# A retention layer's eight sample states: scaled and updated in their own buffers, v spread by one matmul, key tiles added before the query

## What is computed

```python
def step(s, inp):
    qc, kc, vc = inp
    ...
    s = g_c[None, :, None, None] * s + jnp.einsum('bmhk,bmhv->bhkv', kc * zeta[None, :, :, None], vc)
    return s, o
...
mu = jnp.mean(o, axis=-1, keepdims=True)
var = jnp.mean(jnp.square(o - mu), axis=-1, keepdims=True)
o = (o - mu) * lax.rsqrt(var + GN_EPS)
o = o.reshape(B, L, hv) * jax.nn.silu(g.astype(jnp.float32))
return o.astype(xn.dtype) @ w_out, s
```

## Time and profile before

| | us |
|---|---|
| median of 3 runs (2123.94 to 2133.53) | 2125.17 |
| the profiled execution | 2112.8 |
| its span, first to last instruction | 2111.0 |
| TensorE busy, matmuls | 1927.5 (91%) |
| VectorE busy | 1088.6 (52%) |
| ScalarE busy | 813.1 (39%) |
| GpSimd busy | 781.0 (37%) |
| mean granted TensorE clock | 0.938 |

### The profile page before, as it was taken

One profiled execution on the slowest core, in us unless ns is written; L12 is line 12 of the kernel. 1 busy time (PEld: TensorE's weight loads), 2 busy tenths in 40 slices (PEclk: granted clock), 3 DMA queues, 4 the chain that ended last, 5 costly groups with the idle time before them and its releaser, 6 DMA issues.

```text
span 2111.0 us, 32802 instructions
## 1 busy us (share of the span) xinstructions
PE 1927.5 (91%) x14440; PEld 1843.4 (87%) x14440; DVE 1088.6 (52%) x1074; ACT 813.1 (39%) x948; POOL 781.0 (37%) x230
## 2 busy tenths in 40 slices
PE   6989987899966999899999988999999988979998
PEld 6889877899955999898989978999989888879997
DVE  3344543576366764446363544675434544436753
ACT  3332232534425344444344434434532233144343
POOL 4334333545412544342212101355354334253552
PEclk9999997999977999999999978999999999889999
DMA  6657654355623555665454522455556655634452
GB/s 217 198 169 239 225 168 136 120 182 165 192 70 100 169 178 189 191 209 150 135 163 124 148 84 80 136 164 180 180 181 235 231 172 190 200 120 140 161 185 95
DMA packets 305764, 346.86 MB, mean 164 GB/s; under 512 B 7703, under 2 KB 269335, under 8 KB 305615
## 3 DMA queue, kind: packets, MB, share of 16 engines
q1 hardware_dynamic: 257696, 259.84, 38.8%
q10 hardware_dynamic: 47927, 84.93, 12.3%
HBM read 300.17 MB, written 44.82 MB: 163 GB/s over the span
## 4 chain that ended last, share of the span: by engine, by line
PE 80%; DVE 11%; ACT 4%; issue 2%; ACTq 1%; DMA 1%; POOL 0%; DVEq 0%
PE acc L1338 19%; PE acc L1339 19%; PE acc L1345 18%; PE mix L1451 5%; PE mix L1400 2%; PE mix L1442 2%; PE acc L1366 2%; PE acc L1367 1%; ACT w_hi L413 1%; PE acc L1372 1%; PE mix L1681 1%; PE mix L1720 1%; DVE k_stack L1004 1%; DVE w_lo L827 1%; PE mix L1653 1%
## 5 line engine op out<-in xcount | busy, mean ns | idle before, releaser
L1241 POOL TENSOR_TENSOR w_lo<-raw,w_hi 128x2048 fp32r<-128x2048 f32 (+2 forms) x162 | 691.7, 4274 | 886.1 <-ACT w_hi L413 886.1
L1338 PE MATMUL acc<-g_hi,w_hi 128*128 128x264 f32 x2588 | 666.2, 293 | 24.7 <-DVE y L871 11.3
L1339 PE MATMUL acc<-g_lo,w_hi 128*128 128x264 f32 x2588 | 654.4, 289 | 0.0
L413 ACT ACTIVATE w_hi<-raw 128x2048 fp32r<-128x2048 f32 (+3 forms) x260 | 455.7, 1754 | 391.3 <-issue 229.1
L1338 PEld LDWEIGHTS acc<-g_hi,w_hi 128*128 128x128 f32 x2588 | 497.5, 192 | 36.4 <-issue 25.1
L827 DVE TENSOR_TENSOR w_lo<-raw,w_hi 128x2048 fp32r<-128x2048 f32 (+2 forms) x98 | 381.8, 3896 | 272.5 <-ACT w_hi L413 272.3
L1339 PEld LDWEIGHTS acc<-g_lo,w_hi 128*128 128x128 f32 x2588 | 498.5, 193 | 1.4
L1345 PE MATMUL acc<-g_hi,w_lo 128*128 128x264 f32 x2588 | 347.4, 286 | 0.0
L1345 PEld LDWEIGHTS acc<-g_hi,w_lo 128*128 128x128 f32 x2588 | 330.7, 190 | 2.1
L1275 POOL TENSOR_TENSOR h_lo<-hid,h_hi 128x528 fp32r<-128x528 f32 x44 | 59.0, 1342 | 324.6 <-ACT h_hi L608 324.6
L1338 PE MATMUL acc<-h_hi,w_hi 128*128 128x264 f32 x664 | 164.1, 284 | 0.0
(11 more groups left out here) (220 smaller groups left out, 2381.6 us busy)
## 6 DMA issues: line engine op xcount, KB each, us to landing
raw<-in_w_ffn_in_dram SPq DMA_DIRECT2D x88, 1024.0 KB, 5.2
raw<-in_w_in_ret_dram SPq DMA_DIRECT2D x48, 1024.0 KB, 5.6
raw<-in_w_in_attn_dram SPq DMA_DIRECT2D x36, 1024.0 KB, 5.3
st_in<-in_state_ret_dram ACTq DMA_DIRECT2D x64, 512.0 KB, 4.8
out_dram<-st_out ACTq DMA_DIRECT2D x64, 512.0 KB, 3.4
raw<-in_w_ffn_out_dram SPq DMA_DIRECT2D x32, 768.0 KB, 4.3
raw<-in_w_ffn_out_dram SPq DMA_DIRECT2D x32, 640.0 KB, 4.0
raw<-in_w_out_ret_dram SPq DMA_DIRECT2D x16, 1024.0 KB, 5.1
```

The source lines that it names most:

```text
L413: A(w_hi[:, u % SPL, 0:size[u]], raw[:, u % RAW, 0:size[u]], ACT.Copy).then_inc(hi_split, 1)
L1241: TT(w_lo[:, u % SPL, 0:size[u]], raw[:, u % RAW, 0:size[u]], w_hi[:, u % SPL, 0:size[u]].bitcast(F32), ALU.subtract).then_inc(lo_by_pool, 1)
L1338: MM(out, wh, x_hi[:, ks[k], :], start=first and k == 0, stop=False)
L1339: MM(out, wh, x_lo[:, ks[k], :], start=False, stop=False)
```

## The change

st_in and st_out become five buffers `st`, in which a state stays from load to store. ScalarE multiplies it by gamma in place (`scale_to`). TensorE no longer makes k v^T but spreads v of one sample over all partitions with one matmul (`spread`, weights are one column of `sel` broadcast), alternating between the banks mix 2 and 3. VectorE's `update` adds it, times the key as a scalar of each partition (k_s, a copy of 8 columns of rk), for the two key tiles separately. For the query ScalarE multiplies the first key tile by the query's scalar (`t_first`, into the one buffer tq), VectorE adds the second (`t_last`), and TensorE sums tq over the partitions with a column of ones: 4 matmuls of one column instead of 8. A query now goes two samples behind the spread instead of one. k_stack, k_one, the transposes of the k row and v_stack's third and fourth parts are gone. The norm's sums go inside units 4 and 5; head 3's norm is cut into the prompt's 256 columns, which go along with the samples, and the samples' 8 columns ("late"). On ScalarE the hi split of units 4 and 5 comes ahead of the gate's silu, of which the second goes behind the outputs.

```diff
-            st_in = sb("st_in", [P, 3, 2, RDV], F32, s)
-            st_out = sb("st_out", [P, 2, 2, RDV], F32, s)
+            sel = sb("sel", [P, DECB], F32R, s)
+            k_s = sb("k_s", [P, 2, 2, DECB], F32, s)
+            tq = sb("tq", [P, RDV], F32, s)
+            st = sb("st", [P, ST, 2, RDV], F32, s)
...
 ScalarE
+                def load_to(end):
+                    for n in range(loaded[0], min(end, 32)):
+                        g = 32 * r + n
+                        if g >= ST:
+                            act.wait_ge(st_stored[g % ST], 16 * (g // ST))
+                            act.wait_ge(t_ready, g - ST + 1)
+                        act.dma_start(st[:, g % ST], st_view(state_ret, n)).then_inc(st_landed[g % ST], 16)
+                        loaded[0] = n + 1
+                def scale_to(end):
+                    for n in range(grown[0], min(end, 32)):
+                        g = 32 * r + n
+                        act.wait_ge(st_landed[g % ST], 16 * (g // ST + 1))
+                        A(st[:, g % ST], st[:, g % ST], ACT.Copy, scale=GAMMA[n // 8]).then_inc(st_scaled, 1)
+                        grown[0] = n + 1
+                def t_first(n):
+                    g = 32 * r + n
                     act.wait_ge(st_updated, g + 1)
+                    if g:
+                        act.wait_ge(qs_done, g)
+                    b = n % 8
+                    A(tq[:], st[:, g % ST, 0, :], ACT.Copy, scale=rq[:, n // 8 % 2, 0, SEQ + b:SEQ + b + 1])\
+                        .then_inc(t_first_ready, 1)
...
+                    for s in range(4):
+                        n = 8 * (h - 1) + 2 * s
+                        if h:
+                            load_to(n + 4)
                         if h or s:
                             hi(ub + s + 2)
+                        if h:
+                            if s:
+                                t_first(n - 1)
+                            store(n)
+                            load_to(n + 5)
+                            t_first(n)
+                            store(n + 1)
+                            scale_to(n + 4)
...
+                    if h:
+                        t_first(8 * h - 1)
+                    hi(ub + 6)
+                    if h:
+                        sample_out(gh - 1, 1 - par)
+                        load_to(8 * h + 4)
+                        gn_square(h - 1)
+                    gate_out(pb, 4, par)
...
+                    gate_out(pb, 5, par)
+                    act.wait_ge(s1_ready, gh + 1)
+                    act.dma_start(ret_p[r, 0, h].rearrange("(k p) v -> p k v", p=P), S0[:]).then_inc(s1_stored, 16)
+                    if h:
+                        ro_split(h - 1)
+                    scale_to(8 * h + 3)
...
+                    if b == 1:
+                        hi(uo + 2)
+                    if b == 5:
+                        hi(uo + 3)
+                    if b:
+                        t_first(n - 1)
+                    if b == 3:
+                        gn_square(3)
+                    if b == 6:
+                        gn_sqrt(3)
+                    store(n)
+                    load_to(n + 4)
+                    scale_to(n + 3)
...
 VectorE
+                def update(n):
                     g, b = 32 * r + n, n % 8
+                    dve.wait_ge(vb_done, g + 1)
+                    dve.wait_ge(st_scaled, g + 1)
+                    for kt in range(2):
+                        ins = STT(st[:, g % ST, kt, :], mix[:, 2 + g % 2, :], k_s[:, n // 8 % 2, kt, b:b + 1],
+                                  st[:, g % ST, kt, :], ALU.mult, ALU.add)
+                    ins.then_inc(st_updated, 1)
+                def t_last(n):
+                    g, b = 32 * r + n, n % 8
+                    dve.wait_ge(t_first_ready, g + 1)
+                    STT(tq[:], st[:, g % ST, 1, :], rq[:, n // 8 % 2, 1, SEQ + b:SEQ + b + 1], tq[:],
+                        ALU.mult, ALU.add).then_inc(t_ready, 1)
...
+                            update(n)
+                            if s:
+                                t_last(n - 1)
+                            update(n + 1)
+                            t_last(n)
+                        evac(s)
...
+                    if h:
+                        t_last(8 * h - 1)
+                        gn_first(h - 1)
+                        gn_center(h - 1)
+                    evac(4)
+                    if h:
+                        gn_second(h - 1)
+                    dve.wait_ge(v_stack_hi, gh + 1)
+                    TT(v_stack[32:40, :], mix[0:DECB, 2, :], v_stack[0:8, :].bitcast(F32), ALU.subtract)\
+                        .then_inc(v_stack_ready, 1)
+                    if h:
+                        gn_inverse(h - 1)
+                    evac(5)
...
 TensorE
+                def spread(n):
                     g, gh = 32 * r + n, RH * r + n // 8
...
+                    if g > 1:
+                        pe.wait_ge(st_updated, g - 1)
+                    MM(mix[:, 2 + g % 2, :], sel[:, b:b + 1].broadcast_to([P, P]), v_stack[:],
+                       start=True, stop=True).then_inc(vb_done, 1)
+                def query(n):
...
+                    pe.wait_ge(t_ready, g + 1)
+                    for vt in range(4):
+                        ins = MM(mix[:, 0, vt * 8 + b:vt * 8 + b + 1], tq[:, vt * P:(vt + 1) * P], ones[:, 0:1],
                                  start=True, stop=True)
                     ins.then_inc(qs_done, 1)
                 def sample(n):
+                    if n % 8 >= 2:
+                        query(n - 2)
+                    spread(n)
...
+                        if h and s < 4:
+                            samples = (lambda: sample(n), None, lambda: sample(n + 1))
+                        elif h and s == 4:
+                            samples = (lambda: query(8 * h - 1), None, lambda: gn_mean(h - 1))
+                        elif h:
+                            samples = (lambda: gn_variance(h - 1),)
...
+                proj(uo, po, ro_hi, ro_lo, first_half, last=False,
+                     between=(lambda: sample(24), lambda: second(25, gn_mean), lambda: sample(26)))
+                sample(27)
+                proj(uo + 1, po + 1, ro_hi, ro_lo, first_half, last=False,
+                     between=(lambda: sample(28), lambda: second(29, gn_variance), lambda: sample(30)))
+                sample(31)
+                pe.wait_ge(ro_lo_ready, 5 * r + 3)
+                proj(uo + 2, po, ro_hi, ro_lo, pieces[0], first=False, last=False, done=False,
+                     between=(lambda: query(30), None, lambda: query(31)))
+                proj(uo + 3, po + 1, ro_hi, ro_lo, pieces[0], first=False, last=False, done=False,
+                     between=(lambda: gn_mean(3, True), None, lambda: gn_variance(3, True)))
```

386 lines of the change are left out of this document (170 added, 216 removed).

## The result

The changed kernel took 2133.0 us in the median of 17 runs (2122.17 to 2141.35), the kernel before 2122.61 in 17 (2113.86 to 2133.53). The ratio is 1.0044 with a 95% interval of 1.0026 to 1.0062: slower by about 10 us, within the 0.5% (about 11 us) that the prediction called no change, though clear of 1.

What follows compares the result with a forecast made beforehand. TensorE was taken to bound the kernel, with 80% of the last-ending chain. Heads with samples +25, clock +18, first heads -9 and output stages -9 gave +25 us on the median of 2125.17: 2150 us, range 2120 to 2180.

Steps and rivals of the forecast that it cites:

- What decides, the lock: Sample units: t_last, with two SBUF inputs, waits for the end of GpSimd's w_lo under way, stopping TensorE's next query.
- each time: Sample units: t_last(n-1) always comes 0.6 us into a w_lo of 4.58 us.
- The ring, 12.9 us a unit: Units 1 to 3: chain from one blocked query to the next, 12.9 us, hiding TensorE's own 8.1; two layers +25 us.
- Load and gap 0.6: Units 1 to 3, ScalarE: 0.6 us for load issue and gap, counted between the two scalings and the hi split.
- Clock, +18: Heads with samples: after waits, query and spread run at a lower clock; 0 to 6 us a head, 3 taken, +18 us.
- First head with samples: First such head of a layer: no gn_last and ro_split ahead, so 76.8 us against 79.0 for the others.
- First head of a layer, -4.4 each: First head of each layer: the 3.03 us v_stack wait goes, L1521 gains 1.4 at full clock; -4.4 twice, -9 us.
- Output stage, -9: After the heads: two blocked t_last, but a short late norm chain; pieces at 54.5 instead of 58.9, -4.4 twice, -9 us.
- Cost at nothing: Memset of k_stack, k_s copy, and the five state buffers' loads in units 4 and 5: no time lost.
- The first rival: Sample units: t_last is not blocked, units of 8.9 us, heads of 60 us, 2015 us in all; chance 0.15.
- The second rival: Head ends: t_last blocked, but gn_first precedes w_lo (5 us less a head), full clock stays (3 less); 2100 us, chance 0.12.
- The clock stays at its lower level through the sample units: Rival, sample units: TensorE's 8.1 us become 16.2, +3 us for each of 18 units, 2200 us; chance 0.10.

Runs made afterwards that it cites:

- the memset: Changed kernel with GpSimd filling w_lo of the retention layers with zeros instead of subtracting, from the third unit on: 2009.37 us, ratio 0.9474.
- the order: Changed kernel with t_first(n-1) ahead of the hi split in units 1 to 3, nothing else moved: 2062.47 us, ratio 0.973.
- halves: Changed kernel with each w_lo of a retention layer made in two GpSimd instructions of 1024 columns: 2054.77 us, ratio 0.9678.
- quarters: Changed kernel with each w_lo of a retention layer made in four GpSimd instructions of 512 columns: 2023.67 us, ratio 0.9519.
- the norm-first run: Changed kernel with sample_out, and so gn_first, ahead of the hi split in unit 4, nothing else: 2112.71 us, ratio 0.9943.
- eighths: Changed kernel with t_first and sample_out ahead of the hi split everywhere and w_lo in eight parts of 256 columns: 2024.39 us, ratio 0.9563.

## Why the prediction was right and where it was wrong

It said slower, and by 25 us; it was slower by 10. The mechanism was there as described; what failed were sizes, the ring's cost and the output stage's clock. By its own steps:

- **What decides, the lock:** right. 28 of 64 t_last are long and end with a w_lo, and the memset, the order, and the halves and quarters show the cause one by one. Not "each time" at full length, though: a blocked t_last starts 0.57 to 2.5 us into its w_lo, and only 14 take over 4 us. Of the five waits of 3.8 to 5 us a head that were forecast, TensorE shows two in the second head (4.16 and 3.97), one in the third (4.16, then 2.65) and none in the first (2.09 at most). The gn_first that was to be blocked behind the hi of unit 4 is (4.78 us).
- **The ring, 12.9 us a unit:** too long, and this is the step that failed for the heads. Query 1 to query 3 is 12.3 us at full clock. "Load and gap 0.6" does not stand in the chain: the load's issue (171.49) lies inside the first scaling, with ScalarE working beside its own queue; and two scalings are 1.9, not 2.05. From query 0 to query 7 the forecast has 41.2 us at full clock and the trace 40.7, of which some 2.4 are the clock's (next point): about 3 us too much, some 17 over six heads if the ring is the same in all. By milestones from the end of the head before, forecast and measured: query 0 13.5 and 13.0, query 1 21.2 and 20.6, query 3 34.1 and 32.9, query 5 47.0 and 46.4, query 7 54.7 and 53.7, the mean 61.4 and 60.0, end 79.0 and 79.2.
- **Clock, +18:** about right in size in the second head, though its end came out as if the clock had cost nothing. Granted clock of TensorE in that head (stretch, its length, TensorE busy, clock, DMA share, GB/s):

```profile
166.00:180.00 14.00, 9.61 (x76) 0.99 0.69 245
180.00:186.00 6.00, 5.79 (x26) 0.50 0.89 302
186.00:193.60 7.60, 6.44 (x50) 0.96 0.51 175
193.60:201.00 7.40, 5.91 (x45) 1.00 0.82 286
```

  After the wait that ended at 180.21 the clock is at 1.2 GHz, and query 3 takes 1.87 us; after the shorter wait before 193.71 it is at 2.4, and query 5 takes 1.05. So the turn that starts at 180.21 is 13.5 us and the one at full clock 12.3, 1.2 more; this head has two such queries, 0 and 3. At the mean and what follows it come about 1 to 1.6 (17.6 forecast from the mean to the end, 19.2 measured). By this estimate the clock cost 3.4 to 4 us in this head against the 3 taken. With the same ring the first and third heads come to some 4 and 3. In this head the ring was over by as much, and the two hid each other: the end of 79.0 that was forecast at full clock was met at a mean clock of 0.89, and that is luck. The forecast with the clock, 82.0, was not met.
- **First head with samples:** forecast 76.8 before the clock and 79.8 with it, measured 74.7. Beside the ring's surplus query 0 came at 10.1 us (11.3 forecast), and the mean 4.7 us behind query 7 (6.7 forecast; gsq is held for 3.16 us here and not for 4.78). Three heads together: +21 a layer with the clock forecast, +9.7 and +10.5 measured. This is 22 us of the difference: by these estimates some 17 the ring, some 10 what comes before query 0 and between query 7 and the mean, less some 5 that the clock took beyond its +18.
- **First head of a layer, -4.4 each:** -5.1 and -4.5. Right.
- **Output stage, -9:** wrong in sign, +1, and this is the step that failed outside the heads. The clock was charged to the heads and not here, where it was lowest: 0.67 over the stage, with query 24 at 1.84 us. Query 24 came at 13.4 us (15.6 forecast), but query 31 at 53.0 (48), and the chain behind it to the first piece took 9.2 us where 6.5 was forecast. What was mis-sized is the samples between the blocked t_last, not the blocked step: query 24 to 27 took 15.7 us (11.4 forecast) and 28 to 31 16.3 (12.4), where 27 to 28 took 7.6 (8.6). The memset run, with no t_last blocked, has 13.8 and 15.5 for the same. At the lower clock query and spread are 2.5 us instead of 1.4; by that estimate the clock is some 1.1 us a sample, most of the difference. The pieces went at 62.2, not 54.5; what follows them won 2.5 back. This is 10 us the other way.
- **Cost at nothing** (k_s, the memset, the five buffers' loads): right. With t_last out of the way the sample units keep TensorE busy all the time at a DMA share of 0.81.

In sum: 25 - 22 + 10 - 1, about 12, against 11.6 in the two layers. The two wrong steps go opposite ways; that the total is no further off is luck too. The first rival, with no blocked t_last, was put at 2015 us with heads of 60 and rests on the same prices (their sum is 9.0 us a unit, not 8.9): the memset run gave 2009 with heads of 59 to 61. The ranking between it and the forecast was decided by the rows of two SBUF inputs beside a w_lo, and they decided right. The second rival's "gn_first gets in ahead of w_lo" is what the norm-first run made true, and it gave 20 us. "The clock stays at its lower level through the sample units" did not happen.

Where the expected gain of such a change went can now be said: in place, spread and norm sums win 4.5%, and in this order the shorter query costs 4.9%, because its addition is the one new instruction with two SBUF inputs on the path to TensorE, placed behind the start of a 4.5 us instruction of GpSimd, by 0.6 us at the least.

The best that was found is about 5% faster than the kernel before, in two ways that cannot be told apart: the query over two key tiles with sample_out ahead of the split (2015.48 us, 0.9476), or the changed kernel with everything ahead of the split and the w_lo in quarters (2009.83 us, 0.9487). The first is the simpler and has two links fewer between update and query. In the order of the changed kernel, adding the key tiles in PSUM, by the matmul itself, was cheaper than taking them off TensorE; with the lock out of the way the two cannot be told apart.

## What to carry to other kernels

Before work is moved from a saturated engine to an idle one, look at what the idle engine's new instruction reads and what runs on its neighbour at that moment. A VectorE instruction with two SBUF inputs on the critical path must be kept clear of long GpSimd instructions that read SBUF, by its place or by cutting these into a few parts, and not too many. Test such a part by itself: the parts worth 4.5% were hidden here behind one that cost 4.9%.

## What the runs showed of the hardware that was not expected

- **A row of short GpSimd instructions can hold VectorE out for its whole length**: 15.34 us for a 0.70 us sum, twice in one run, in a row that begins with 256-wide parts; in one of 512-wide parts 0.81 at the same place. It isn't so of every row: with everything ahead of the split, five t_last that met a w_lo with the next one right behind it got in between (2.19 us at 153.94, for one), and that next w_lo took some 5.0 us instead of 4.6.
- **A scalar operand from SBUF is not a second input.** The update L994 reads one bank of PSUM, one state tile and a column of k_s. It never waited, though 58 of the 128 had a w_lo or a ro_lo beside them:

```profile
L994 DVE SCALAR_TENSOR_TENSOR st<-mix,k_s,st x128: 740/744/754, 75.4 to 1867.4; 128x512 f32<-128x512 f32 x128
```

- **Cutting a GpSimd instruction costs little at first**: a 2048-wide w_lo takes 4.5 to 4.6 us, and in the trace with quarters GpSimd is busy 824.8 us in all against 780.1, with eighths 857.1.
- **A low clock costs only what stands in the chain.** After the waits of 4.16 and 3.97 us the granted clock was 0.50 for some 6 us each, and after one of 2.65 us in the third head 0.72 over 6 us. After 3.97 us at 180.21 some 1.2 us of what ran slowly reached the next query of the chain; the rest lay inside idle time.
